# The last chunk of two streamed tensors (H's sixteenth, G's eleventh) starts 64 bytes further on

## The chip, the cores and the metric

The kernel runs on one core of a Trainium2 chip. The metric is the device time of one execution in microseconds (us); less is better. Engines are TensorE (PE in the profile, its weight loads PEld), VectorE (DVE), ScalarE (ACT), GpSimd (POOL) and SyncE (SP), which issues the weight transfers.

## The reference

A sequence of 256 tokens of width 2048 goes through two blocks of two layers each, in float32. What matters here is that nearly all of the arithmetic is products of the 2048-wide activations with large weight matrices:

```python
def first_block(x, p, positions, ...):
    for i in range(DEPTH):
        h = rmsnorm(x, g_mix[i])
        z = h @ w_in[i]
        ...
        y = jnp.concatenate([y_a, y_b, y_c, y_d], axis=-1) @ w_o[i]
        x = x + y
        uf = causal_dwconv(rmsnorm(x, g_ffn[i]) @ w_up[i], w_ffn_conv[i])
        gate, up = jnp.split(uf, 2, axis=-1)
        x = x + (jax.nn.silu(gate) * up) @ w_down[i]
        pe_gate = jax.nn.sigmoid(rmsnorm(x, g_pe[i]) @ w_pg[i])
        x = x + (p[i] @ w_pe[i]) * pe_gate
    return x
```

Between `w_in` and `w_o` stand an attention, a gated convolution, a longer convolution and a retention; their 512-wide outputs are joined. The second block (`hybrid_layer`) has the same frame: a norm, one projection `w_in`, four mixers (three kinds of attention and a gated linear attention) and `w_out`. It ends with a norm of x.

## The kernel before

Activations lie with channels on the 128 partitions: a tensor of 2048 channels is 16 chunks (`DC`) of 128 channels by T = 256 tokens. To get float32 precision, each operand is split in two parts in the type float32r, a high part and the remainder. `H` holds the operand of the current product, 16 chunks of 512 columns: columns 0 to 255 of a chunk are its high part (written by ScalarE, L1226, L1236, L1338, L1356 or L1502) and columns 256 to 511 the low part (written by VectorE, L1686 or L1697). `G` holds the same for the gated FFN activation, two buffers of 11 chunks (`GC`); its parts are written by ScalarE (L1564) and GpSimd (L514).

Weights come in slabs, one slab for each 128 output channels: 16 blocks (11 for `down`) of 128 x 128. SyncE loads a slab into `raw`, a ring of 4; ScalarE copies it to `whi` (L1164); VectorE writes the remainder to `wlo` (L1630), which takes the place of `raw`. TensorE goes through the slabs one after another. `run` is the loop over the slabs of one product. For each slab of the kind `streams_both` it does two passes over the chunks into one PSUM bank: in the first, block k of `whi` is the loaded weight and all 512 columns of chunk k are streamed (L642); in the second, block k of `wlo` is loaded and the 256 high columns are streamed (L653). Each matmul has its own weight load. Then VectorE adds the bank's halves and takes the result out, while TensorE is at the next slab. The first two slabs behind a norm are done in another order by `high_first` (L585, L587: whi and wlo blocks in turn on the high part; L596: whi on the low part, 32 in a row). `value_slab` (L676 to L678) loads pieces of `H` as weights and streams `whi` and `wlo`. `both_units` (L703 to L707) streams `pT_hl` in halves of 256 columns, with whi, whi and wlo in turn, right ahead of the product `pg`. Small matmuls of the attentions are put between the slabs of `zq` to `rg` and `gla` to `gates`, and ahead of the last quarter of their first pass.

The product `wout` takes its chunks in the order `Y_ORDER[1]` (0 to 9, 12 to 15, 10, 11), that is how they come ready; the parameter `order` of `run` hands it over (L631, L649).

SBUF is laid out in the order of the allocations. Three unused tensors stand between them and shift what follows: `ahead_of_raw` (320 bytes a partition), `ahead_of_whi` (192 bytes) and `ahead_of_z` (416 bytes). A chunk of H or G is 2048 bytes, a weight block 512 bytes. In the built program the start addresses in a partition are H 32896, raw and wlo 65984, whi 98944, pT_hl 149312, G and z 179840, cq 212608. By "line parity" the change means whether such an address divided by 64 is even or odd.

Of the kernel before, what the change touches and what calls it, by code (L numbers as in the profile page):

```python
# [27 lines left out]
P = 128  # L28
T = 256
# [226 lines left out]
def _build(nc, d, out, ctx):  # L256
    def sb(name, shape, dt=F32):
        return ctx.enter_context(nc.sbuf_tensor(name, shape, dt))
# [3 lines left out]
    H = sb("H", [P, DC, 2 * T], F32R)  # L262
    sb("ahead_of_raw", [P, 80])
# [48 lines left out]
    G = ctx.enter_context(nc.sbuf_tensor("G", [P, 2, GC, 2 * T], F32R))  # L312
    ctx.enter_context(nc.sbuf_tensor("rest_of_y", [P, 48 * T - 2 * GC * 2 * T], F32))
# [148 lines left out]
    def _(pool):  # L462
# [36 lines left out]
        def activations(l, g):  # L499
# [4 lines left out]
            for i, j in groups(pool, r, 2):  # L504
# [8 lines left out]
                gg = G[:, g % 2, bass.ds(pair, 1), :].rearrange("p a t -> p (a t)")  # L513
# [49 lines left out]
    def _(pe):  # L563
# [6 lines left out]
        def high_first(key, h_base, order, middle):  # L570
# [4 lines left out]
            for u in range(2):  # L575
# [5 lines left out]
                for k in chunks:  # L581
# [3 lines left out]
                    pe.matmul(b[:, 0:T], whi[:, n % RAW, w], r.src[:, k, 0:T], start=k == chunks[0], stop=False,  # L585
                              skip_group_check=True)
                    pe.matmul(b[:, 0:T], wlo[:, n % RAW, w], r.src[:, k, 0:T], start=False, stop=k == chunks[-1],  # L587
                              skip_group_check=True)
            middle()
            for u in range(2):  # L590
                n = r.first + u
                b = bank_of(r, n)
                for k in chunks:
                    if u == 0:
                        pe.wait_ge(S("h_ready"), h_base + rank[k] + 1)
                    last = pe.matmul(b[:, T:2 * T], whi[:, n % RAW, k * r.m:(k + 1) * r.m], r.src[:, k, T:2 * T],  # L596
# [3 lines left out]
        def run(key, operand=None, beside=None, base=None, free=None, order=None, high=None, middle=None):  # L600
# [5 lines left out]
            for i, j in groups(pe, r, 0):  # L606
# [21 lines left out]
                for first in range(0, r.kt, step):  # L628
                    chunks = range(first, min(first + step, r.kt))
                    for at in chunks:  # L630
                        k = at if order is None else order[at]  # L631
# [9 lines left out]
                        if both:  # L641
                            pe.matmul(b[0:r.m, :], whi[:, n % RAW, w], r.src[:, k, :], start=at == 0, stop=False)  # L642
                        else:
                            pe.matmul(b[0:r.m, 0:T], whi[:, n % RAW, w], r.src[:, k, 0:T], start=at == 0, stop=False)
                            pe.matmul(b[0:r.m, 0:T], whi[:, n % RAW, w], r.src[:, k, T:2 * T], start=False, stop=False)
                    if both and not opening and first == 0:
                        pe.wait_ge(S("lo_ready"), n + 4 * i + 1)
                    for at in chunks:
                        k = at if order is None else order[at]  # L649
# [3 lines left out]
                        last = pe.matmul(b[0:r.m, 0:T], wlo[:, n % RAW, w], r.src[:, k, 0:T], start=False,  # L653
# [8 lines left out]
        def value_slab(r, g):  # L662
# [5 lines left out]
            for kk in range(4):  # L668
# [4 lines left out]
                for t in range(2):  # L673
                    b = bank_of(r, n0 + t)
                    high, low = (r.src[:, k, o + t * P:o + (t + 1) * P] for o in (0, T))
# [13 lines left out]
        def both_units(l):  # L689

            r = by["pe", l]
            for u in range(2):
                n = r.first + u
                pe.wait_ge(S("lo_ready"), n + 1)
                for p in range(4):
# [3 lines left out]
                    for o in range(2):  # L699
                        dst = b[:, o * T:(o + 1) * T]  # L700
                        for k in range(2):
                            w = slice(8 * P * k + P * (2 * p + o), 8 * P * k + P * (2 * p + o + 1))
                            pe.matmul(dst, whi[:, n % RAW, w], r.src[:, k, 0:T], start=k == 0, stop=False,  # L703
# [1579 lines left out]
```

## Time and profile before

| | us |
|---|---|
| median of 3 runs | 3352.53 (3350.43 to 3353.65) |
| profiled execution | 3352.41 |
| its span in the trace | 3350.2 |
| PE busy in the span | 3327.6 (99%) |
| DVE busy | 2617.8 (78%) |
| ACT busy | 1531.6 (46%) |
| POOL busy | 864.2 (26%) |

The profile page gives busy times, shares in 40 equal slices, the waits, and the costliest groups of instructions by line of the kernel. Matmuls overlap one another: each takes longer from its start to its end than the next one's start lags behind its own. So a group's mean says little of the pace; the timeline does. It merges instructions of the same kind into one row with the start of the first, the time from there to the end of the last, and their count. A window that is cut short shows the first few of a longer row.

### The profile page before, as it was taken

Reading aid. Unit: us, or ns where it says so; the run is one execution under the profiler, and the core shown is the slowest. Engines: PE = TensorE matmul, PEld = TensorE weight load, DVE = VectorE, ACT = ScalarE, POOL = GpSimd, SP = SyncE. Lnnn points to the kernel's source line nnn. Section 1 sums busy time; section 2 is a strip of 40 time slices with the busy share of each in tenths; the row PEclk is TensorE's granted clock in tenths of the full one; section 3 lists DMA queues with packets and bytes.
Section 4 is the critical chain, followed back from the end, with each engine's and each line's share of the span. In section 5 each row is a group of like instructions: output and inputs, shape, how many; then the busy total and the mean of one; then the engine's idle time right before and its main releaser. Section 6 shows DMA issues by size and latency. Waiting matters only on the chain. (4 is left out here: it accounts for less than half of the span.)

```text
span 3350.2 us, 53769 instructions
## 1 busy us (share of the span) xinstructions
PE 3327.6 (99%) x20366; PEld 2929.1 (87%) x20366; DVE 2617.8 (78%) x3394; ACT 1531.6 (46%) x1642; POOL 864.2 (26%) x633
## 2 busy tenths in 40 slices
PE   9999999999999999999999999999999999999998
PEld 8989888888888989888888888888888888888897
DVE  8897788787786888887887787867867866678865
ACT  5644444343433556544443434335444444445443
POOL 0422432121122423414332121214432004150004
PEclk9999999999999999999999999999999999999999
DMA  6445555555555554455555555555544455544454
GB/s 241 148 163 176 189 188 189 178 202 177 206 174 189 203 182 165 151 176 187 190 188 178 198 180 199 180 190 200 193 164 153 167 173 189 180 164 151 167 185 151
DMA packets 90647, 605.21 MB, mean 181 GB/s; under 512 B 10192, under 2 KB 10352, under 8 KB 29296
## 3 DMA queue, kind: packets, MB, share of 16 engines
q1 hardware_dynamic: 89424, 599.83, 52.0%
q10 hardware_dynamic: 1056, 3.11, 0.2%
q8 instruction: 110, 1.80, 0.2%
q14 instruction: 57, 0.47, 0.0%
HBM read 600.80 MB, written 2.10 MB: 180 GB/s over the span
## 5 line engine op out<-in xcount | busy, mean ns | idle before, releaser
L642 PE MATMUL bank<-H,whi 128*128 128x512 f32 x6496 | 1574.3, 393 | 1.5 <-DVE z L1661 1.5
L1164 ACT ACTIVATE whi<-raw 128x2048 fp32r<-128x2048 f32 (+2 forms) x609 | 1093.6, 1796 | 1044.6 <-DMA raw<-in_slabs_down 259.8
L1630 DVE TENSOR_TENSOR wlo<-raw,whi 128x2048 fp32r<-128x2048 f32 (+2 forms) x609 | 1328.4, 2181 | 243.2 <-ACT whi L1164 233.1
L642 PEld LDWEIGHTS bank<-H,whi 128*128 128x128 f32 x6496 | 1188.7, 188 | 238.6 <-issue 5.9
L653 PEld LDWEIGHTS bank<-H,wlo 128*128 128x128 f32 x6624 | 849.1, 188 | 34.3
L653 PE MATMUL bank<-H,wlo 128*128 128x256 f32 x6624 | 871.1, 281 | 0.0
L511 POOL TENSOR_TENSOR sqtmp<-tmp 128x256 f32<-128x256 f32 x88 | 218.9, 2488 | 867.8 <-DVE tmp L2211 867.8
L642 PE MATMUL bank<-G,whi 128*128 128x512 f32 x1408 | 343.0, 391 | 0.0
L642 PEld LDWEIGHTS bank<-G,whi 128*128 128x128 f32 x1408 | 255.4, 188 | 48.0
L1564 ACT ACTIVATE G<-sqtmp 128x256 f32 (+1 forms) x88 | 36.8, 418 | 404.0 <-POOL sqtmp L511 404.0
L489 POOL TENSOR_TENSOR sqacc<-sqacc,sqtmp 128x256 f32<-128x256 f32 x119 | 199.4, 1676 | 9.4
L1651 DVE TENSOR_REDUCE tmp<-bank 128x256 f32<-128x512 f32 x216 | 149.0, 690 | 65.9 <-PE bank L653 65.4
L484 POOL TENSOR_TENSOR sqtmp<-x 128x256 f32<-128x256 f32 x119 | 133.7, 1123 | 238.5 <-DVE x L1705 182.5
L653 PEld LDWEIGHTS bank<-G,wlo 128*128 128x128 f32 x1408 | 184.3, 189 | 9.8
L529 POOL TENSOR_TENSOR z<-z,y 128x255 f32<-128x255 f32 (+14 forms) x120 | 121.1, 1009 | 269.9 <-ACT y L1381 254.2
L1704 DVE TENSOR_TENSOR x<-x,bank 128x256 f32 (+1 forms) x192 | 80.7, 420 | 138.8 <-PE bank L653 138.7
L653 PE MATMUL bank<-G,wlo 128*128 128x256 f32 x1408 | 186.8, 281 | 0.0
L1651 DVE TENSOR_REDUCE z<-bank 128x256 f32<-128x512 f32 x132 | 91.0, 690 | 103.1 <-PE bank L653 102.0
L484 POOL TENSOR_TENSOR sqacc<-x 128x256 f32<-128x256 f32 x8 | 16.3, 2031 | 589.0 <-DVE x L1705 547.1
L676 PE MATMUL bank<-whi,H 128*128 128x512 f32 x320 | 129.9, 406 | 0.0
L678 PE MATMUL bank<-whi,H 128*128 128x512 f32 x320 | 126.1, 394 | 0.0
L677 PE MATMUL bank<-wlo,H 128*128 128x512 f32 x320 | 126.0, 394 | 0.0
(390 smaller groups left out, 2881.4 us busy)
## 6 DMA issues: line engine op xcount, KB each, us to landing
raw<-in_slabs_up SPq DMA_DIRECT2D x176, 1024.0 KB, 4.8
raw<-in_slabs_down SPq DMA_DIRECT2D x128, 704.0 KB, 4.0
raw<-in_slabs_wo SPq DMA_DIRECT2D x32, 1024.0 KB, 4.8
raw<-in_slabs_pg SPq DMA_DIRECT2D x32, 1024.0 KB, 4.9
raw<-in_slabs_gates SPq DMA_DIRECT2D x32, 1024.0 KB, 4.9
raw<-in_slabs_wout SPq DMA_DIRECT2D x32, 1024.0 KB, 4.8
raw<-in_slabs_sc SPq DMA_DIRECT2D x24, 1024.0 KB, 4.8
raw<-in_slabs_fox SPq DMA_DIRECT2D x24, 1024.0 KB, 4.9
```

The source lines that it names most:

```text
L484: pool.tensor_tensor((sqtmp if c else sqacc)[:], x[:, c, :], x[:, c, :], ALU.mult).then_inc(S("pool_sq"), 1)
L489: ins = pool.tensor_tensor(sqacc[:], sqacc[:], sqtmp[:], ALU.add)
L511: pool.tensor_tensor(act_f[:], tmp[:, 3, :], tmp[:, 2, :], ALU.mult).then_inc(S("act_f32"), 1)
L529: pool.tensor_tensor(o[:, s:T], o[:, s:T], product[:, done["tap"] % TAP_RING, s:T], ALU.add).then_inc(S("cf_pool"), 1)
L642: pe.matmul(b[0:r.m, :], whi[:, n % RAW, w], r.src[:, k, :], start=at == 0, stop=False)
L653: last = pe.matmul(b[0:r.m, 0:T], wlo[:, n % RAW, w], r.src[:, k, 0:T], start=False, stop=at == r.kt - 1)
L676: pe.matmul(b[:], high, whi[:, n % RAW, w], start=k == 0, stop=False)
L677: pe.matmul(b[:], high, wlo[:, n % RAW, w], start=False, stop=False)
L678: last = pe.matmul(b[:], low, whi[:, n % RAW, w], start=False, stop=k == DC - 1)
L1164: act.activation(whi[:, n % RAW, 0:w], raw[:, n % RAW, 0:w], ACT.Copy).then_inc(S("hi_ready"), 1)
L1630: dve.tensor_tensor(wlo[:, n % RAW, 0:w], raw[:, n % RAW, 0:w], whi[:, n % RAW, 0:w].bitcast(F32), ALU.subtract).then_inc(S("lo_ready"), 1)
L1651: return dve.tensor_reduce(dst, b[0:m, :].rearrange("p (h t) -> p t h", h=2), AX, ALU.add)
```

## The change

H and G lose their last chunk, which becomes a tensor of its own behind 64 unused bytes (16 float32). The pad behind H shrinks by the same 64 bytes, so raw, wlo, whi and all that follows stay where they were; the 64 bytes behind G come out of the unused rest of that area. H's chunk 15 starts at byte 63680 instead of 63616, and G's chunk 10 at 220864 and 222912. G's second buffer of ten chunks starts at 200320 instead of 202368. H becomes a list of chunks, and `r.src[:, k, ...]` is written `r.src[k][:, ...]` in all its uses; `g_chunk` picks a chunk of G. The slabs of `wo` and `wout` behind the first two no longer follow `order`, but go through the chunks from 0 to 15; for `wo` this is the same. The count of instructions, their sizes and their waits stay.

```diff
--- before.py
+++ after.py
@@ -259,8 +259,11 @@
 
 
     x = sb("x", [P, DC, T])
-    H = sb("H", [P, DC, 2 * T], F32R)
-    sb("ahead_of_raw", [P, 80])
+    H_most = sb("H", [P, DC - 1, 2 * T], F32R)
+    sb("ahead_of_H_last", [P, 16])
+    H_last = sb("H_last", [P, 2 * T], F32R)
+    H = [H_most[:, c, :] for c in range(DC - 1)] + [H_last[:]]
+    sb("ahead_of_raw", [P, 64])
     area_raw = nc.sbuf_tensor("raw", [P, RAW, 2048], F32)
     raw = area_raw.__enter__()
     area_raw.__exit__(None, None, None)
@@ -309,8 +312,16 @@
     cq = area_cq.__enter__()
     area_cq.__exit__(None, None, None)
     area.__exit__(None, None, None)
-    G = ctx.enter_context(nc.sbuf_tensor("G", [P, 2, GC, 2 * T], F32R))
-    ctx.enter_context(nc.sbuf_tensor("rest_of_y", [P, 48 * T - 2 * GC * 2 * T], F32))
+    G = sb("G", [P, 2, GC - 1, 2 * T], F32R)
+    sb("ahead_of_G_last", [P, 16])
+    G_last = sb("G_last", [P, 2, 2 * T], F32R)
+    sb("rest_of_y", [P, 48 * T - 2 * GC * 2 * T - 16])
+
+    def g_chunk(g, pair):
+
+        if isinstance(pair, int):
+            return G_last[:, g % 2, :] if pair == GC - 1 else G[:, g % 2, pair, :]
+        return G[:, g % 2, bass.ds(pair, 1), :].rearrange("p a t -> p (a t)")
 
     bank = [ctx.enter_context(nc.psum_tensor(f"bank{b}", [P, 512], F32)) for b in range(4)]
     pS = ctx.enter_context(nc.psum_tensor("pS", [P, 512], F32))
@@ -339,13 +350,14 @@
 
     HANDED = ("wo", "pg", "wout", "rg", "gates")
     runs, by, h_free = [], {}, {}
-    sources = {"qn": cq, "qr": cq, "kv": cq[:, 4:6, :]}
+    latent = [cq[:, c, :] for c in range(6)]
+    sources = {"qn": latent[0:4], "qr": latent[0:4], "kv": latent[4:6]}
     for key, _, _, kt, m, count, _, _ in slab_table():
         src = sources.get(key[0], H)
         if key[0] == "down":
-            src = G[:, key[2] % 2]
+            src = [g_chunk(key[2], c) for c in range(GC)]
         elif key[0] == "pe":
-            src = pT_hl[:, key[1]]
+            src = [pT_hl[:, key[1], c, :] for c in range(2)]
         loop = key[0] in ("wo", "up", "down", "pg", "wout")
         by[key] = Run(d[slab_name(key)], kt, m, count, src, loop, sum(r.count for r in runs))
         if key[0] in ("pg", "wo", "wout") or key[0] == "up" and key[2] == 0:
@@ -510,7 +522,7 @@
                 pool.wait_ge(S("g_ready"), 1 + base + pair)
                 pool.tensor_tensor(act_f[:], tmp[:, 3, :], tmp[:, 2, :], ALU.mult).then_inc(S("act_f32"), 1)
                 pool.wait_ge(S("g_hi"), base + pair + 1)
-                gg = G[:, g % 2, bass.ds(pair, 1), :].rearrange("p a t -> p (a t)")
+                gg = g_chunk(g, pair)
                 pool.tensor_tensor(gg[:, T:2 * T], act_f[:], gg[:, 0:T].bitcast(F32),
                                    ALU.subtract).then_inc(S("g_ready"), 1)
 
...
@@ -628,7 +640,7 @@
                 for first in range(0, r.kt, step):
                     chunks = range(first, min(first + step, r.kt))
                     for at in chunks:
-                        k = at if order is None else order[at]
+                        k = at
                         if opening and at == 0:
                             pe.wait_ge(S("h_ready"), 8)
                         if opening and at % 4 == 0:
...
@@ -639,18 +651,18 @@
                             operand(k)
                         w = slice(k * r.m, (k + 1) * r.m)
                         if both:
-                            pe.matmul(b[0:r.m, :], whi[:, n % RAW, w], r.src[:, k, :], start=at == 0, stop=False)
+                            pe.matmul(b[0:r.m, :], whi[:, n % RAW, w], r.src[k], start=at == 0, stop=False)
                         else:
-                            pe.matmul(b[0:r.m, 0:T], whi[:, n % RAW, w], r.src[:, k, 0:T], start=at == 0, stop=False)
-                            pe.matmul(b[0:r.m, 0:T], whi[:, n % RAW, w], r.src[:, k, T:2 * T], start=False, stop=False)
+                            pe.matmul(b[0:r.m, 0:T], whi[:, n % RAW, w], r.src[k][:, 0:T], start=at == 0, stop=False)
+                            pe.matmul(b[0:r.m, 0:T], whi[:, n % RAW, w], r.src[k][:, T:2 * T], start=False, stop=False)
                     if both and not opening and first == 0:
                         pe.wait_ge(S("lo_ready"), n + 4 * i + 1)
                     for at in chunks:
-                        k = at if order is None else order[at]
+                        k = at
                         w = slice(k * r.m, (k + 1) * r.m)
                         if at == (r.kt // 4 if step == r.kt else r.kt * 6 // 8):
                             advance(beside, 1)
-                        last = pe.matmul(b[0:r.m, 0:T], wlo[:, n % RAW, w], r.src[:, k, 0:T], start=False,
+                        last = pe.matmul(b[0:r.m, 0:T], wlo[:, n % RAW, w], r.src[k][:, 0:T], start=False,
                                          stop=at == r.kt - 1)
                         if handed and at in (3, 7, 11):
                             last.then_inc(S("h_free"), 1)
...
@@ -1683,7 +1695,7 @@
             h0 = DC * ((cnt["h"] if lo else nth("h")) - 1)
             for c in range(lo, hi):
                 dve.wait_ge(S("h_hi"), h0 + c + 1)
-                dve.scalar_tensor_tensor(H[:, c, T:2 * T], x[:, c, :], col(g, l, c), H[:, c, 0:T].bitcast(F32),
+                dve.scalar_tensor_tensor(H[c][:, T:2 * T], x[:, c, :], col(g, l, c), H[c][:, 0:T].bitcast(F32),
                                          ALU.mult, ALU.subtract).then_inc(S("h_ready"), 1)
 
         def scaled(dst, b, m=P):
```

The other hunks put `r.src[k][:, ...]` for `r.src[:, k, ...]`, `H[c][:, ...]` for `H[:, c, ...]` and `g_chunk(...)` for an indexed G in the same way.

## Rows read from the trace of the kernel before

**Rows 1.** The page's head, busy shares, and granted clock in 40 slices.
```profile
span 3350.2 us, 53769 instructions
PE 3327.6 (99%) x20366; PEld 2929.1 (87%) x20366; DVE 2617.8 (78%) x3394; ACT 1531.6 (46%) x1642; POOL 864.2 (26%) x633
...
PEclk9999999999999999999999999999999999999999
```

**Rows 2.** Waits of PE, the longest: total us, times, longest us.
```profile
PE pX L1085 <- ACT whi L1520: 5.0, 1, 5.0
```

**Rows 3.** The page's groups of L642 and L653: count, busy us, mean ns.
```profile
L642 PE MATMUL bank<-H,whi 128*128 128x512 f32 x6496 | 1574.3, 393 | 1.5 <-DVE z L1661 1.5
...
L653 PE MATMUL bank<-H,wlo 128*128 128x256 f32 x6624 | 871.1, 281 | 0.0
...
L642 PE MATMUL bank<-G,whi 128*128 128x512 f32 x1408 | 343.0, 391 | 0.0
```

**Rows 4.** Timeline of PE, one slab on H: start us, length us, line, count.
```profile
1803.26 3.82 PE L642 MATMUL bank<-H,whi 128*128 128x512 f32 x16
1806.91 2.05 PE L653 MATMUL bank<-H,wlo 128*128 128x256 f32 x16
1808.80 2.68 PE L642 MATMUL bank<-G,whi 128*128 128x512 f32 x11
```

**Rows 5.** Timelines of PE and PEld in windows that cut this first pass short.
```profile
1803.26 1.55 PE L642 MATMUL bank<-H,whi 128*128 128x512 f32 x6
...
1803.26 2.23 PE L642 MATMUL bank<-H,whi 128*128 128x512 f32 x9
...
1803.14 1.00 PEld L642 LDWEIGHTS bank<-H,whi 128*128 128x128 f32 x5
```

**Rows 6.** Timeline of PE behind high_first: L596 and the slab after it.
```profile
291.90 4.00 PE L596 MATMUL bank<-H,whi 128*128 128x256 f32 x32
295.74 3.82 PE L642 MATMUL bank<-H,whi 128*128 128x512 f32 x16
299.39 0.28 PE L653 MATMUL bank<-H,wlo 128*128 128x256 f32 x1
```

**Rows 7.** Timeline of PE behind both_units, in three windows; the last is layer 1.
```profile
1116.92 0.28 PE L707 MATMUL pX<-pT_hl,wlo 128*128 128x256 f32 x1
1117.04 3.79 PE L642 MATMUL bank<-H,whi 128*128 128x512 f32 x16
1120.66 2.05 PE L653 MATMUL bank<-H,wlo 128*128 128x256 f32 x16
...
1117.04 2.20 PE L642 MATMUL bank<-H,whi 128*128 128x512 f32 x9
...
2307.97 3.79 PE L642 MATMUL bank<-H,whi 128*128 128x512 f32 x16
```

**Rows 8.** Timeline of the other engines at 1803 and at 1117.
```profile
1802.99 1.36 ACT L1164 ACTIVATE whi<-raw 128x1408 fp32r<-128x1408 f32 x1
...
1803.46 0.69 DVE L1651 TENSOR_REDUCE tmp<-bank 128x256 f32<-128x512 f32 x1 [1.43 <-PE bank L653]
...
1116.51 1.92 ACT L1164 ACTIVATE whi<-raw 128x2048 fp32r<-128x2048 f32 x1
...
1117.48 0.68 DVE L2219 COPY z<-bank 128x512 f32<-128x512 f32 x1
```

**Rows 9.** Busy us of each engine in 300 us of up and down.
```profile
1700.00:2000.00 300.00, 300.00 (x1736) 265.02 (x1735) 242.50 (x307) 118.69 (x103) 72.27 (x44) 1.00 0.54 187
```

**Rows 10.** Timeline of PE, a second pass behind a first pass cut by attention matmuls.
```profile
206.15 1.18 PE L642 MATMUL bank<-H,whi 128*128 128x512 f32 x4
207.17 1.99 PE L653 MATMUL bank<-H,wlo 128*128 128x256 f32 x16
```

**Rows 11.** Timeline of PE behind a value slab.
```profile
185.19 3.79 PE L642 MATMUL bank<-H,whi 128*128 128x512 f32 x16
188.82 2.05 PE L653 MATMUL bank<-H,wlo 128*128 128x256 f32 x16
```

More of the change, by code:

```diff
@@ L584, in high_first @@
                     w = slice(k * r.m, (k + 1) * r.m)
-                    pe.matmul(b[:, 0:T], whi[:, n % RAW, w], r.src[:, k, 0:T], start=k == chunks[0], stop=False,
+                    pe.matmul(b[:, 0:T], whi[:, n % RAW, w], r.src[k][:, 0:T], start=k == chunks[0], stop=False,
                               skip_group_check=True)
-                    pe.matmul(b[:, 0:T], wlo[:, n % RAW, w], r.src[:, k, 0:T], start=False, stop=k == chunks[-1],
+                    pe.matmul(b[:, 0:T], wlo[:, n % RAW, w], r.src[k][:, 0:T], start=False, stop=k == chunks[-1],
                               skip_group_check=True)
@@ L595, in high_first @@
                         pe.wait_ge(S("h_ready"), h_base + rank[k] + 1)
-                    last = pe.matmul(b[:, T:2 * T], whi[:, n % RAW, k * r.m:(k + 1) * r.m], r.src[:, k, T:2 * T],
+                    last = pe.matmul(b[:, T:2 * T], whi[:, n % RAW, k * r.m:(k + 1) * r.m], r.src[k][:, T:2 * T],
                                      start=k == chunks[0], stop=k == chunks[-1], skip_group_check=True)
@@ L674, in value_slab @@
                     b = bank_of(r, n0 + t)
-                    high, low = (r.src[:, k, o + t * P:o + (t + 1) * P] for o in (0, T))
+                    high, low = (r.src[k][:, o + t * P:o + (t + 1) * P] for o in (0, T))
                     pe.matmul(b[:], high, whi[:, n % RAW, w], start=k == 0, stop=False)
@@ L702, in both_units @@
                             w = slice(8 * P * k + P * (2 * p + o), 8 * P * k + P * (2 * p + o + 1))
[L703 removed]
+                            pe.matmul(dst, whi[:, n % RAW, w], r.src[k][:, 0:T], start=k == 0, stop=False,
                                       skip_group_check=True)
[L705 removed]
+                            pe.matmul(dst, whi[:, n % RAW, w], r.src[k][:, T:2 * T], start=False, stop=False,
                                       skip_group_check=True)
[L707 removed]
+                            last = pe.matmul(dst, wlo[:, n % RAW, w], r.src[k][:, 0:T], start=False, stop=k == 1,
                                              skip_group_check=True)
@@ L744, in pair_unit @@
                         w = slice(r.m * k + P * (2 * p + o), r.m * k + P * (2 * p + o + 1))
-                        pe.matmul(dst, whi[:, n % RAW, w], r.src[:, k, 0:T], start=k == 0, stop=False,
+                        pe.matmul(dst, whi[:, n % RAW, w], r.src[k][:, 0:T], start=k == 0, stop=False,
                                   skip_group_check=True)
-                        pe.matmul(dst, whi[:, n % RAW, w], r.src[:, k, T:2 * T], start=False, stop=False,
+                        pe.matmul(dst, whi[:, n % RAW, w], r.src[k][:, T:2 * T], start=False, stop=False,
                                   skip_group_check=True)
-                        last = pe.matmul(dst, wlo[:, n % RAW, w], r.src[:, k, 0:T], start=False, stop=k == r.kt - 1,
+                        last = pe.matmul(dst, wlo[:, n % RAW, w], r.src[k][:, 0:T], start=False, stop=k == r.kt - 1,
                                          skip_group_check=True)
```

16 lines of the change are left out of this document (7 added, 9 removed).

## The prediction, made before the kernel after was run

> **What bounds the kernel now.** I read the page's busy shares first, then the waits of TensorE, then its costliest groups, then its timeline in narrow windows, then the timeline of all engines. The shares say TensorE: 3327.6 of 3350.2 us busy, the next engine at 78%, the granted clock in the top tenth in every slice (so 2.4 GHz but for the first and last microseconds) [rows 1]. Its longest wait on anybody is 5.0 us, once [rows 2]. So only what one matmul costs in the stream of matmuls can move the time. The groups name the stream: per slab 16 matmuls of 512 columns with weights from whi (I call it the high pass) and 16 of 256 columns with weights from wlo (the low pass), 11 and 11 where G is streamed; 6496/16 = 406 such slabs on H and 1408/11 = 128 on G, 534 in all [rows 3]. The means in these rows (393, 281 ns) overlap one another; what counts is start to start, which the timeline gives.
>
> **One slab, start to start.** A high pass on H starts at 1803.26 and its low pass at 1806.91: 3.65 us for 16. The low pass ends at the next start, 1808.80: 1.89 us for 16, 118 ns each [rows 4]. The high pass isn't even. Its first six span 1.55 us; a row ends 0.39 us after its last start (the row that ends with the pass: 3.82 us long, next start after 3.65, and a mean of 0.39 in the groups), so five steps take 1.16 us, 232 ns each. The other eleven take 3.65 - 1.16 = 2.49 us, 226.4 ns each [rows 3 to 5]. So every high pass pays about 5 x (232 - 226.5) = 0.027 us at its start. That is 0.03 us that steady streaming doesn't need.
>
> **What the change touches.** It adds no instruction, no wait and no transfer. In the built program of before H starts at byte 32896, wlo at 65984, whi at 98944, pT_hl at 149312, G at 179840, cq at 212608; divided by 64 these are even, odd, even, odd, even, even, and chunks (2048 or 1024 bytes) and weight blocks (512 bytes) keep their tensor's parity. The change makes H's chunk 15 and G's chunk 10 odd; everything else stays where it was or keeps its parity. The weight load of matmul k+1 starts with the stream of matmul k: the first whi load of the pass at 1803.26 starts at 1803.14, one low step ahead of it [rows 5]. So each stream runs beside a load, and a pair can have the same parity or different ones:
> - high pass, chunks 0 to 14: H even, whi even: same. Low pass, chunks 0 to 14: H even, wlo odd: different. Unchanged.
> - last of the high pass, beside the first wlo load: different before, same after.
> - last of the low pass, beside the next slab's first whi load: same before, different after.
> - chunk 14 beside the load for chunk 15: unchanged, the weights don't move.
>
> So the change makes each pass keep its own relation up to its last matmul. The order argument that it drops in wout's later slabs also makes the last chunk there 15 instead of 11, so those slabs take part too; their waits are unchanged, cost 0.
>
> **Does the parity matter?** The trace has two passages that are near to the changed one.
> - 32 matmuls of 256 columns on H with whi weights (same parity, L596) take 295.74 - 291.90 = 3.84 us, 120.0 ns each; the low pass with wlo weights takes 118 [rows 4, 6]. So a same-parity pair costs about 2 ns more at this width. Behind them the high pass again takes 3.65 us (295.74 to 299.39): slow start.
> - Behind the pT_hl unit the last 256-column stream is odd beside an even whi load, which is exactly the pair that the change makes. There the high pass takes 1120.66 - 1117.04 = 3.62 us, and its first nine span 2.20 us where the ordinary one's span 2.23 [rows 5, 7]. The slow start is gone; the second pT_hl unit, in the other layer, shows the same. Both stretches have the same neighbours: VectorE reads the bank just finished and ScalarE writes whi at 1803 and at 1117 alike [rows 8]. So the slow start isn't their doing, and goes with what streamed last.
>
> Sum. High pass: 3.65 - 3.62 = 0.03 us by the rows; 0.027 by the steps above. Last low matmul: 120 to 118, 0.002. Last high matmul turns from different to same: bound by the same 2 ns as a loss, 0.001 taken. So 0.027 to 0.03, taken 0.028 us for each high pass that follows directly on a low pass ending in the moved chunk. Counting these through the timeline of the span gives 319 behind H and 126 behind G, 445 of 534; the others have attention matmuls ahead of them, or are cut in fours, and keep what they have. 445 x 0.028 = 12.5 us. Cover: none is needed, TensorE is the bound; VectorE is busy 242.5 us of 300 in an up/down stretch [rows 9], so 0.4% less TensorE time doesn't make it late. The profiled run took 3352.41 us around a span of 3350.2, and the median of before is 3352.53, 0.12 more. 3352.4 - 12.5 = **3340 us**.
>
> **The unobserved side.** No passage of before has a 512-column stream in a same-parity pair directly ahead of a low pass. What this does to the low pass has to be bounded from both sides, and the low pass is sensitive: behind a high pass of four that is itself still in its slow start, 16 low matmuls span 1.99 us instead of 2.05 [rows 4, 10], (1.99 - 0.28)/15 = 114.0 ns each instead of 118.0. So there are at least two steady paces, and which one is caught hangs on how the pass is entered. Upper bound: the pace of L596, 120, or a slow start like the high pass's. I take zero, because the low pass starts at 118 now after a high pass that is steady when it ends, and a last high matmul that stays steady resembles that most.
>
> **A rule against.** By the rows, 256-column steps of 120 and 118 ns differ only in which weights are loaded beside them. The Trainium skill (TensorE: Matmul & The Clock Gate, "Part 2: What happens when you issue a matmul") says that the engine reads the stream and the weights through two independent ports, and that loading the next weights takes nothing from the running matmul; by that rule alone the change is worth 0 and the sum 3352.4. It is rival 1, and the 2 ns and the 0.03 us speak against it as far as two passages can.
>
> **Rivals.**
> 1. No effect, or trading one slow start for another (20%): the slow start is a property of entering 512 columns from 256, and the pT_hl unit escapes it since it mixes weights and halves. For it: all 445 passes are entered in that one way, and the pT_hl unit is met only twice. Against: the high pass behind a value slab, entered from a same-parity 512-column stream, takes 188.82 - 185.19 = 3.63 us [rows 11], and the one behind L596, all one kind of weights, still has the slow start, so the last stream does matter. Time: 3352, or 3347 to 3357 with small changes.
> 2. The low pass gets worse (slower, 22%): the last high stream now shares its parity with the first wlo load, and the low pass goes at L596's pace. Price: 2 ns x 16 x about 396 + 2 ns x 11 x 128 = 15.5 us; or a slow start of 0.028 us x 524 = 14.7 us. With the gain kept: 3352.4 - 12.5 + 15 = 3355. With the gain missing: 3367. It decides from 12.5/524 = 24 ns per slab, 1.5 ns per low matmul, on. I give 6% to the two cancelling (within 0.2%), 16% to slower by over 0.2%.
> 3. The low pass falls into the pace of 114 (9%): 4 ns x 16 x 396 + 4 ns x 11 x 128 = 31 us beyond the gain: 3309; half of the slabs, 3325.
> 4. The sum itself, 3334 to 3345: 49%.
>
> **How the numbers follow.** Likeliest 3340. What can be told from no change here is about 0.2%, 6.7 us: faster below 3345.7, slower above 3359.1. Faster: 49 + 9 + 1 of rival 1 = 59%. Slower: 16 + 2 of rival 1 = 18%. Same: the rest, 23%. The range runs from 3324, which takes in half of rival 3, to 3360, which takes in rival 1 and the cancelling part of rival 2; the rest of rival 3 and of rival 2 stay out, some 19%. The likeliest case alone is 3334 to 3345.
>
> **What the profile after would show.** Right: ordinary high passes of 3.62 us instead of 3.65, their first nine spanning 2.20; the low pass still 1.88 to 1.89 us; the group rows of L642 with the same counts; the saving spread over all stretches by their number of slabs and largest in up and down. Rival 1: 3.65 stays. Rival 2: low passes at 1.91 to 1.92 or an uneven start in them. Rival 3: low passes at 1.82. What would make me wrong: the parity isn't what the chip sees (another address bit), or the odd chunk behind an even one (or the even one behind an odd one) costs something of its own, twice per pass, in which case steps 14 to 15 and 15 to 0 are long; 6 ns each would take back the whole gain.

## The result, and the profile after

The kernel after takes 3358.78 us (median of 21 runs, 3356.62 to 3363.3) against 3352.09 for the kernel before, run beside it. The ratio is 1.0021, 95% interval 1.0014 to 1.0027: slower by 0.2%, where I forecast 0.4% faster. The profiled execution took 3358.79 us around a span of 3356.6, 6.4 us more than the span of before.

Part of the scatter from execution to execution is TensorE's granted clock. Beside the f runs below, before took 3350.1 us (median of 10) at a mean clock of 0.999 and 3352.3 (median of 17) at 0.998. In its profiled execution the clock was 0.66 from 116 to 121 us, so it stood at 1.2 GHz in part of that window, and the matmuls there took 5.97 us where they took 4.41 in after. After has two such places, at 144 to 149 and at 1328 to 1333 us, also 0.66.

TensorE is still the bound, and nothing new waits. The head of the page, busy shares and granted clock:

```profile
span 3356.6 us, 53769 instructions
PE 3335.2 (99%) x20366; PEld 2927.2 (87%) x20366; DVE 2616.7 (78%) x3394; ACT 1531.5 (46%) x1642; POOL 866.2 (26%) x633
...
PEclk9999999999999999999999999999999999999999
```

The longest waits of PE (total us, times, longest us):

```profile
PE pX L1097 <- ACT whi L1532: 5.1, 1, 5.1
PE pX L944 <- POOL w L561: 3.1, 6, 0.8
```

Counts, slices of the clock and the longest wait are those of [rows 1] and [rows 2], within 0.1 us; lines from 640 on have moved by 12, so L654 and L665 are the high and the low pass. The loss is in the steps. The timeline of PE, one ordinary slab on H and one on G (start us, length us, line, count); the moved chunk now has a row of its own:

```profile
1801.74 3.61 PE L654 MATMUL bank<-H,whi 128*128 128x512 f32 x15
1805.18 0.39 PE L654 MATMUL bank<-H_last,whi 128*128 128x512 f32 x1
1805.41 1.93 PE L665 MATMUL bank<-H,wlo 128*128 128x256 f32 x15
1807.18 0.28 PE L665 MATMUL bank<-H_last,wlo 128*128 128x256 f32 x1
1807.30 3.61 PE L654 MATMUL bank<-H,whi 128*128 128x512 f32 x15
...
1812.86 2.47 PE L654 MATMUL bank<-G,whi 128*128 128x512 f32 x10
1815.17 0.39 PE L654 MATMUL bank<-G_last,whi 128*128 128x512 f32 x1
1815.40 1.34 PE L665 MATMUL bank<-G,wlo 128*128 128x256 f32 x10
1816.58 0.28 PE L665 MATMUL bank<-G_last,wlo 128*128 128x256 f32 x1
1816.69 2.45 PE L654 MATMUL bank<-G,whi 128*128 128x512 f32 x10
```

On H the high pass takes 1805.41 - 1801.74 = 3.67 us where [rows 4] has 3.65, and the slab 1807.30 - 1801.74 = 5.56 where [rows 4] has 5.54. Windows that cut the pass short show where:

```profile
1801.74 1.55 PE L654 MATMUL bank<-H,whi 128*128 128x512 f32 x6
...
1801.74 2.25 PE L654 MATMUL bank<-H,whi 128*128 128x512 f32 x9
```

Six span 1.55 us as in [rows 5], but nine span 2.25 instead of 2.23: the slow start is not gone, it lasts longer. Start to start, the median over the 291 ordinary high passes on H, worked out from the whole timeline of each kernel, in ns:

```
before  233 236 228 232 231 227 227 227 227 227 227 227 ... 227 226
after   232 233 236 224 231 236 228 233 231 227 227 227 ... 227 232
```

The sequence 231, 236, 228, 232 or 233, 231, 227 is the same in both; only the first step differs from it in before. After enters it four steps earlier, which costs 16 ns a pass, and its last step takes 232 ns instead of 226. The low pass is 2 ns shorter. So a slab of H takes 20 ns more. On G the last high step costs 6 ns more too, but the last low step takes 113 ns instead of 118, and the slow start is unchanged: 3.813 us a slab in both.

One more loss lies where attention matmuls cut the high pass and its last four matmuls run in the slow start. The low pass behind them, timeline of PE of after:

```profile
206.91 1.93 PE L665 MATMUL bank<-H,wlo 128*128 128x256 f32 x15
208.68 0.28 PE L665 MATMUL bank<-H_last,wlo 128*128 128x256 f32 x1
```

(1.93 - 0.28)/14 = 118 ns a step, where [rows 10] had 114. There are 36 such passes; 34 had the pace of 114 in before and 10 have it in after, so 24 lost it, at 0.05 us each 1.2 us. Moving the last high stream of H is enough for that: in e5 below, where nothing else moves, 10 of the 36 have it too, and in e1, where only the last low stream moves, 34.

The estimate by units is 319 x 0.020 = 6.4 us on H, 0 on G and 1.2 in the cut passes, 7.6; the span grew by 6.4. Step by step over the whole span, matmul for matmul, the difference divides so: H's other passes +5.8 us, G's +0.1, the cut low passes +1.2, the places with a lower clock +1.5 (two instead of one), 42 steps of over 0.4 us -0.8, and all other matmuls -1.5; 6.3 in sum.

### The profile page after: what moved, and what is told of

Same layout as the page of the kernel before. It is cut to its first block and busy times, and to the rows that moved or that the text cites. A ratio compares the mean times of both kernels' runs of the same rounds, so it can differ in the third digit from the quotient of the medians.

```text
span 3356.6 us, 53769 instructions
## 1 busy us (share of the span) xinstructions
PE 3335.2 (99%) x20366; PEld 2927.2 (87%) x20366; DVE 2616.7 (78%) x3394; ACT 1531.5 (46%) x1642; POOL 866.2 (26%) x633
## 5 line engine op out<-in xcount | busy, mean ns | idle before, releaser
L654 PE MATMUL bank<-H,whi 128*128 128x512 f32 (+1 forms) x6090 | 1486.8, 394 | 1.2 <-ACT whi L1176 0.4
L654 PEld LDWEIGHTS bank<-H,whi 128*128 128x128 f32 (+1 forms) x6090 | 1110.4, 188 | 228.6 <-issue 3.9
L665 PEld LDWEIGHTS bank<-H,wlo 128*128 128x128 f32 (+1 forms) x6210 | 801.7, 189 | 36.6
L665 PE MATMUL bank<-H,wlo 128*128 128x256 f32 (+1 forms) x6210 | 822.3, 281 | 0.0
L654 PE MATMUL bank<-G,whi 128*128 128x512 f32 x1280 | 314.2, 391 | 0.0
L654 PEld LDWEIGHTS bank<-G,whi 128*128 128x128 f32 x1280 | 230.8, 188 | 43.1
L665 PEld LDWEIGHTS bank<-G,wlo 128*128 128x128 f32 x1280 | 169.0, 189 | 10.5
L665 PE MATMUL bank<-G,wlo 128*128 128x256 f32 x1280 | 171.4, 281 | 0.0
L654 PE MATMUL bank<-H_last,whi 128*128 128x512 f32 (+1 forms) x406 | 159.5, 393 | 0.0
L688 PE MATMUL bank<-whi,H 128*128 128x512 f32 x300 | 122.0, 407 | 0.0
L690 PE MATMUL bank<-whi,H 128*128 128x512 f32 x300 | 118.2, 394 | 0.0
```

Source lines behind the costliest of these rows:

```text
L654: pe.matmul(b[0:r.m, :], whi[:, n % RAW, w], r.src[k], start=at == 0, stop=False)
L665: last = pe.matmul(b[0:r.m, 0:T], wlo[:, n % RAW, w], r.src[k][:, 0:T], start=False, stop=at == r.kt - 1)
L688: pe.matmul(b[:], high, whi[:, n % RAW, w], start=k == 0, stop=False)
L690: last = pe.matmul(b[:], low, whi[:, n % RAW, w], start=False, stop=k == DC - 1)
```

## The experiments

In the e runs and in g2 the layout stays that of before, but for e4, e5 and e8, and a single stream of each pass (in e3 every stream of the low pass) is started at another address by taking it some columns later or earlier in the tensor. These kernels (not e4 and e8) compute with shifted data. The time of a step doesn't show that: the last high step takes 232 ns in e5 as in after, and 237 in e2 as in f3, where the data are the right ones. The f runs and g1 are after with other shifts. `flat` is H, or G's buffer, as one row of columns; 16 columns are 64 bytes.

### Each moved place alone: e1 and e2

```diff
 e1: low pass
-last = pe.matmul(..., r.src[:, k, 0:T], ...)
+last = pe.matmul(..., flat[:, 512 * k + s:512 * k + s + T], ...)   # s = 16 if at == r.kt - 1 else 0
 e2: high pass
-pe.matmul(..., r.src[:, k, :], ...)
+pe.matmul(..., flat[:, 512 * k + s:512 * k + s + 512], ...)        # s = -16 if at == r.kt - 1 else 0
```

> The layout of before; only the last matmul of each low pass (chunk 15 of H, chunk 10 of G, 256 columns) streams from 64 bytes further on, so that its start is odd; the data streamed there are shifted by 16 columns. Theory A (the two moved streams act each by itself, and the odd last low stream is what enters H's high pass earlier in its slow start): ordinary H high passes take 3.67 us instead of 3.65, their last step stays at 226 ns, G's last low step falls to 113 ns; 319 x 0.016 us = +5 us on H, 128 x 0.005 = 0.6 us less on G, together 3356 to 3357. Rival B (the longer slow start comes from the last high stream, through the phase that the low pass inherits): high passes stay at 3.65 us and the time at 3352 or 0.6 us less. The theory of the prediction (the odd last low stream removes the slow start): high passes of 3.62 us, 3340.

Measured: 3354.14 us, ratio 1.0009 (1.0000 to 1.0019). The odd last low stream alone gives H a slab of 5.540 us, the same as before, though by other steps: the last low step takes 122 ns instead of 120 and the next high pass starts 230, 224, 231, 236, 228. On G it enters the slow start where after has it on H (232, 233, 236, 224, ...), 3.833 us a slab. So theory A had the mechanism on the wrong tensor. Rival B's forecast holds for the length of H's high pass (3.652 us), but not for its steps and not on G. The prediction's own theory falls: no ordinary high pass lost its slow start. The 2.4 us that e1 takes more than before (3351.71, run beside it) are G's: 126 x 0.020 = 2.5.

> The layout of before; only the last matmul of each high pass (512 columns) streams from 64 bytes further back, so that its start is odd; the data streamed there are shifted by 16 columns. Theory A: its step takes 232 ns instead of 226, nothing else moves: 534 x 0.0056 = +3.0 us, 3355. Rival B: the step of 232 and, behind the low pass, a high pass that starts earlier in its slow start, 3.67 us before its last step: 3.0 + 4.5 = 7.5 us, 3360, so that this one place explains the whole loss.

Measured: 3355.60 us, ratio 1.0012 (1.0002 to 1.0021). The last high step takes 237 ns, not 232, and behind the low pass the next high pass starts with 231 instead of 233 on H. Neither expectation fits: 64 bytes back isn't 64 bytes on. H's slab takes 5.547 us.

### Steady parity: e3 and e4

```diff
 e3: low pass, every chunk
+last = pe.matmul(..., flat[:, 512 * k + 16:512 * k + 16 + T], ...)
 e4: layout
+sb("ahead_of_H", [P, 16])
 H = sb("H", [P, DC, 2 * T], F32R)
-sb("ahead_of_raw", [P, 80])
+sb("ahead_of_raw", [P, 64])
```

> The layout of before; every matmul of each low pass streams from 64 bytes further on (data shifted by 16 columns), so that all its starts are odd like the wlo blocks loaded beside them. If same parity costs 2 ns at this width in itself (the reading of L596): low steps of 120 ns, 7904 x 2.3 ns = +18 us, 3370. If the L596 pace came from something else (whi blocks, the low half streamed): low steps stay at 117.5 and the time within 3350 to 3357. If what cleared the slow start behind pT_hl was a run of odd streams and not one: high passes of 3.62 us here, 12 us less than either.

Measured: 3365.64 us, ratio 1.0047 (1.0030 to 1.0063). The timeline of PE in e3:

```profile
1804.42 3.82 PE L647 MATMUL bank<-H,whi 128*128 128x512 f32 x16
1808.08 2.07 PE L658 MATMUL bank<-H,wlo 128*128 128x256 f32 x16
1809.99 3.37 PE L647 MATMUL bank<-H,whi 128*128 128x512 f32 x14
```

The low pass takes 1.91 us instead of 1.89; from its seventh step on each takes 120 ns. The reading of L596 holds, somewhat less than priced because the first six steps are uneven (116 to 121). The high pass takes 3.66: a run of odd streams doesn't clear the slow start either.

> H as a whole is moved on by 64 bytes, G, raw, wlo and whi stay where they are; nothing is left out. High passes on H then pair odd streams with even whi loads, low passes odd streams with odd wlo loads. If the parity of stream and load sets the pace: high steps of 224 ns instead of 226.7 (the pace of a last step, 225.8, or less) and low steps of 120 instead of 117.5, in sum 406 x 16 x (2.3 - 0.9 to 2.7) ns: between 3350 and 3361, with G's passes as before. If only changes of parity between one stream and the next matter: H's passes keep 226.7 and 117.5 with the slow start unchanged, 3352 within 2 us.

Measured: 3366.40 us, ratio 1.0044 (1.0027 to 1.0061). Low steps on H take 120 ns. High steps go 226, 229, 232 in turn, 229 on average against 226.7, with no slow start at all, 3.660 us a pass. At 256 columns the four pairs are now complete. Stream even beside load even (L596) takes 120 ns and odd beside odd (the low passes of e3 and e4) 120 too; even beside odd (low pass of before) takes 117.5 and odd beside even (e4's L597, which is L596 of before) 118. So there the pair decides, and not the address of the stream alone. For steady high passes only two pairs were run, both with whi even: the same-parity pair of before is better by 2.3 ns. The layout of before has the better one of both widths. That the high step would get shorter was wrong. The 225.8 ns of a last high step isn't the pace of such pairs, it is a single step out of step.

### Does parity decide? e5, e6, e7

```diff
 e5: H with 16 spare columns, ahead_of_raw 16 shorter; high pass on H only
+pe.matmul(..., H_flat[:, 512 * k + s:512 * k + s + 512], ...)      # s = 16 if at == r.kt - 1 else 0
 e6, e7: as e1 with s = 32 (128 bytes) and s = 8 (32 bytes)
```

> The layout of before; only on H, the last matmul of each high pass streams from 64 bytes further on, as after does (in e2 it was 64 bytes back, and its step took 237 ns where after's takes 232). Data shifted by 16 columns. If the two moves act each by itself: the last high step takes 232 ns, +2.3 us over 406 slabs, the next high pass starts as before (233, 236, 228, 232, 231 ns), and e5 and e1 add up to after: 3354.5. If they act through the phase that the low pass hands on: the last low step or the first high steps change too, by some 2 to 16 ns per slab, up or down, and the sum of e1 and e5 isn't after. If 64 back and 64 on are the same to the chip (parity alone decides), the last step takes 237 ns again.

Measured: 3353.02 us, ratio 1.0003 (0.9994 to 1.0013). The last high step takes 232 ns as in after, the low pass is 4 ns shorter, and the next high pass starts with 231 instead of 233. H's slab: 5.540 us, as before. So on H neither move alone costs a slab anything, and both together cost 20 ns. The last low step and the next high pass change here although their own addresses don't: something is handed on from step to step.

> As e1_low_last with 128 bytes instead of 64, so that the last low stream starts even again (data shifted by 32 columns). If line parity is what the chip sees: steps and high passes of before (last low step 120 ns on H, 118 on G; high passes start 233, 236 on H and 231, 236 on G). If the length of the jump or a higher address bit matters: other values.

Measured in one run: 3351.88 us. The start is even again, and yet H's high pass enters its slow start late (232, 232, 231, 227) and takes 3.641 us, and G's enters it early and takes 2.539. The timeline of PE in e6:

```profile
1803.28 3.80 PE L647 MATMUL bank<-H,whi 128*128 128x512 f32 x16
1806.92 2.05 PE L658 MATMUL bank<-H,wlo 128*128 128x256 f32 x16
1808.81 2.67 PE L647 MATMUL bank<-G,whi 128*128 128x512 f32 x11
```

Line parity alone isn't what decides at the last step of a pass.

> As e1_low_last with 32 bytes: the start lies in the middle of a line, and 17 lines are touched. If only the parity of the line of the first byte matters: the steps of before. If the place in the line matters: last low step between 118 and 124 ns and the next high pass entered at another point of its slow start, -5 to +18 ns per slab.

Measured in one run: 3354.99 us. H's last low step takes 125 ns and the high pass starts 224, 231, 236; the slab again takes 5.540 us. The place in the line matters for single steps; over the slab it comes out even. (The 3354.99 is no sign of more: the mean clock of this execution was 0.997, and that of before took 3355.5 us at 0.997, median of three beside it.)

### The passage that the prediction rested on: e8

```diff
+sb("ahead_of_pT", [P, 16])
 pT_hl = sb("pT_hl", [P, L, 2, 2 * T], F32R)
+sb("behind_pT", [P, 48])
...
-sb("ahead_of_z", [P, 104])
+sb("ahead_of_z", [P, 40])
```

> Only pT_hl moves on by 64 bytes (tensors between it and z by 256, z and all else stay); nothing is left out. It tests the step of the prediction on which the gain stood. If the odd last stream behind both_units was what spared the next high pass its slow start, that pass now takes 3.65 us like the others. If it was something else in that passage (streams of whi, whi and wlo in turn), it still takes 3.62 us. The time is that of before in both cases, since there are only two such passes.

Measured in one run: 3351.28 us. The timeline of PE in e8, then the same place in after, where pT_hl is odd as it was before:

```profile
1115.31 0.28 PE L709 MATMUL pX<-pT_hl,wlo 128*128 128x256 f32 x1
1115.43 3.81 PE L644 MATMUL bank<-H,whi 128*128 128x512 f32 x16
1119.08 1.10 PE L655 MATMUL bank<-H,wlo 128*128 128x256 f32 x8
```

and in after:

```profile
1118.65 0.28 PE L719 MATMUL pX<-pT_hl,wlo 128*128 128x256 f32 x1
1118.77 3.60 PE L654 MATMUL bank<-H,whi 128*128 128x512 f32 x15
1122.21 0.39 PE L654 MATMUL bank<-H_last,whi 128*128 128x512 f32 x1
1122.44 0.75 PE L665 MATMUL bank<-H,wlo 128*128 128x256 f32 x5
```

With pT_hl even the pass has its slow start, 3.65 us: the line did matter there. But in after, with pT_hl odd as in [rows 7], the pass also has a slow start and takes 3.67. So an odd last stream clears it in one course of steps and not in another. What sets the course lies further back. In f1 below, which differs from after only in G's last chunk, the slow start is absent again, in both layers; the timeline of PE in f1:

```profile
1118.53 0.28 PE L718 MATMUL pX<-pT_hl,wlo 128*128 128x256 f32 x1
1118.65 3.56 PE L653 MATMUL bank<-H,whi 128*128 128x512 f32 x15
1122.05 0.39 PE L653 MATMUL bank<-H_last,whi 128*128 128x512 f32 x1
1122.28 0.99 PE L664 MATMUL bank<-H,wlo 128*128 128x256 f32 x7
```

The high pass takes 1122.28 - 1118.65 = 3.63 us, 6 ns of it the longer last step. Between G's last low stream and this pass lie the 96 matmuls of both_units, some 11 us, with the same addresses in both kernels. Their steps run through one repeating series from 114 to 124 ns, and the pass meets it at another point: the last steps ahead of it are 118, 117, 121, 116 in f1 and 117, 116, 119, 114 in after. The other runs agree: the pass is free of the slow start in before, e5, f1, f4 and g3, where G's last low stream is unmoved or 256 on, and has it in e1, e3, e7, f2, f3, g1 and g2, where it is moved. Only e6 doesn't fit this, where it is moved by 128 and the pass stays free. (Counted by the first of the two such passes in e1 and g1, whose second starts with a longer step; e2, e4 and e8 are left out.)

### After with other shifts: f1 to f4, g1

```diff
 f1: H 64 bytes, G 0      f2: both 128      f3: both 192      f4: both 256      g1: H 128, G 192
-sb("ahead_of_H_last", [P, 16])
+sb("ahead_of_H_last", [P, h])
-sb("ahead_of_raw", [P, 64])
+sb("ahead_of_raw", [P, 80 - h])
-sb("ahead_of_G_last", [P, 16])
+sb("ahead_of_G_last", [P, g])
```

> After with G's last chunk put back to an even line (its two last chunks stay a tensor of their own behind the others). H's chunk 15 stays 64 bytes on. If H alone brings the loss: slabs of H as in after (high pass 3.675 us, low pass 1.885), slabs of G as in before (2.518 and 1.296), and the time is after's, 3358 to 3360, since G's slabs took 3.81 us in both. If the jump to the chunk matters rather than its line (G's buffer 0 now jumps over buffer 1), G's last steps change by some ns although every start is even.

Measured: 3359.76 us, ratio 1.0021 (1.0012 to 1.0030), the whole loss. H's slabs are those of after, G's those of before, although G's first buffer now jumps over its second to reach its last chunk. H alone makes the loss, and the jump's length doesn't show in the ordinary slabs.

> After with both last chunks 128 bytes on instead of 64: all starts are even again. If line parity is what the chip sees, all steps are those of before and the time is 3352. If the bytes count beyond parity, as e6 showed for the low pass alone (H's high pass 3.641 us instead of 3.653, G's 2.539 instead of 2.518), other values: with the low pass's effect alone, H gains 0.013 us x 319 and G loses 0.021 us x 126, 3351; the last high step, not measured at 128, moves by 0 to 6 ns, 0 to +3 us, and shifts where the low pass's pattern ends, 5540 ns a slab plus or minus 20: 3345 to 3360.

Measured: 3346.64 us, ratio 0.9980 (0.9971 to 0.9989): faster than before. The timeline of PE in f2, whole and in a window that cuts the pass short:

```profile
1798.42 3.56 PE L654 MATMUL bank<-H,whi 128*128 128x512 f32 x15
1801.82 0.40 PE L654 MATMUL bank<-H_last,whi 128*128 128x512 f32 x1
1802.05 1.93 PE L665 MATMUL bank<-H,wlo 128*128 128x256 f32 x15
1803.82 0.28 PE L665 MATMUL bank<-H_last,wlo 128*128 128x256 f32 x1
1803.94 2.43 PE L654 MATMUL bank<-G,whi 128*128 128x512 f32 x10
...
1798.42 1.52 PE L654 MATMUL bank<-H,whi 128*128 128x512 f32 x6
```

Six span 1.52 us where [rows 5] has 1.55: here H's slow start is gone (226 or 227 ns from the first step on). It gives 28 ns a pass; the last high step, 234 ns, takes back 8. The slab takes 5.520 us.

> After with both last chunks 192 bytes on: all parities are those of after. If line parity decides, every step and the time are after's: last high step 232 ns, H's high pass 3.675 us, 3358.8. If not, a slab of H takes something else than 5.560 us (5.520 to 5.570 by what the other shifts gave) and the time lies between 3344 and 3362.

Measured: 3356.04 us, ratio 1.0015 (1.0006 to 1.0024). H's slab takes 5.560 us as in after, with a last high step of 237, the same as in e2, and -64 and 192 differ by 256. G's slow start is gone instead of H's: 3.800 us a slab.

> After with both last chunks 256 bytes on: all parities are those of before. If 256 bytes are a period of what the chip sees, or parity alone counts, every step is that of before (high pass 233, 236, 228, 232, 231 ns first, last step 226, low pass ending in 120), 3352. If the jump itself costs, whatever its length, the last step of the high pass is longer than 226 ns and the time above 3353.

Measured: 3352.18 us, ratio 1.0000 (0.9991 to 1.0009), with every step of the ordinary slabs within 1 ns of before (233, 236, 228, 233, 231 first, 226 last). For this stream 256 bytes on are as good as none, and splitting the tensors costs nothing.

> After with H's last chunk 128 bytes on and G's 192, each the best shift that the runs so far show for its tensor. If a slab's time depends only on its own tensor's shift: H as in f2 (5.520 us a slab), G as in f3 (2.506 + 1.294 = 3.800 us against 3.813 in f2), so 128 x 0.013 = 1.7 us less than f2, 3345. If passes of H and G disturb one another where they meet, G's gain is missing or H's smaller: 3347 to 3352.

Measured: 3345.36 us, ratio 0.9980 (0.9971 to 0.9989), the fastest kernel here; its profiled span is 3341.3 against 3343.5 in f2. The timeline of PE in g1:

```profile
1796.87 3.56 PE L654 MATMUL bank<-H,whi 128*128 128x512 f32 x15
1800.26 0.40 PE L654 MATMUL bank<-H_last,whi 128*128 128x512 f32 x1
1800.50 1.93 PE L665 MATMUL bank<-H,wlo 128*128 128x256 f32 x15
...
1802.38 2.43 PE L654 MATMUL bank<-G,whi 128*128 128x512 f32 x10
1804.65 0.40 PE L654 MATMUL bank<-G_last,whi 128*128 128x512 f32 x1
1804.89 1.34 PE L665 MATMUL bank<-G,wlo 128*128 128x256 f32 x10
1806.07 0.28 PE L665 MATMUL bank<-G_last,wlo 128*128 128x256 f32 x1
1806.18 2.43 PE L654 MATMUL bank<-G,whi 128*128 128x512 f32 x10
```

A slab of G takes 1806.18 - 1802.38 = 3.80 us, and H keeps its 5.520: the ordinary slabs of the two tensors don't disturb one another. The timed difference to f2, 1.3 us, is within the scatter of both; at a mean clock of 0.999 the medians of three executions each are 3343.5 and 3345.1, 1.6 apart where 1.7 was expected.

### What was left: g2 and g3

```diff
 g2: as e1 with s = 48 (192 bytes)
 g3: before, in run, both passes
-k = at if order is None else order[at]
+k = at
```

> The layout of before; only the last stream of each low pass starts 192 bytes further on (data shifted by 48 columns). It separates the two places for the shift that takes G's slow start away in f3. If the last low stream does it alone: G's high pass 2.50 us here too, H's 3.67 or so as in f3. If it takes both places together, through the pattern of the low pass: G's and H's high passes are other than in f3, as e6 (G 2.539, H 3.641) differs from f2 (2.515, 3.633).

Measured in one run: 3346.05 us. With the last low stream alone at 192, it is H whose slow start goes (one step of 233, then 227), 5.520 us, and G has an early entry, 3.827. In f3, with both places at 192, it was the other way round. It takes both places together.

> Before with only the order of wout's later slabs dropped, the one part of the change that no other run has alone: the last chunk there is 15 instead of 11, both even, and chunks 10 and 11 are no longer behind 15. If it costs nothing, as the prediction had it: 3352 and wout's high passes at 3.653 us. If the jump back and forth or the last chunk's place matters: wout's 28 slabs change by up to 20 ns each, 0.6 us, still within what can't be told from no change.

Measured: 3351.80 us, ratio 1.0002 (0.9993 to 1.0012); the ordinary high passes take 3.653 us. The dropped order has no part in the loss.

### The shifts in one table

Medians over the ordinary passes and slabs, in ns, worked out from the timelines; "last" is the last step. The slab is taken from start to start of two high passes. f1 is after on H and before on G, g1 is f2 on H and f3 on G.

| run | moved, bytes | H high (last) | H low (last) | H slab | G slab |
|---|---|---|---|---|---|
| before, f4 | 0, both 256 | 3653 (226) | 1887 (120) | 5540 | 3813 |
| e5 | H high 64 | 3657 (232) | 1883 (118) | 5540 | 3813 |
| e1 | low 64 | 3652 (226) | 1888 (122) | 5540 | 3833 |
| after | both 64 | 3675 (232) | 1885 (120) | 5560 | 3813 |
| e7 | low 32 | 3648 (226) | 1892 (125) | 5540 | 3813 |
| e6 | low 128 | 3641 (226) | 1886 (119) | 5527 | 3833 |
| f2 | both 128 | 3633 (234) | 1887 (119) | 5520 | 3813 |
| g2 | low 192 | 3632 (226) | 1888 (121) | 5520 | 3827 |
| e2 | high -64 | 3662 (237) | 1884 (118) | 5547 | 3827 |
| f3 | both 192 | 3676 (237) | 1884 (118) | 5560 | 3800 |

## Why the prediction was wrong

- **TensorE is the bound, and only steps can move the time:** right. No count changed, and the two longest waits of PE stayed at 5.0 to 5.1 and 3.1 to 3.4 us. (A misreading without weight: the clock was below 2.4 GHz near 118 us too, which 40 slices are too coarse to show.)
- **A same-parity pair costs 2 ns in the low pass:** right for a whole pass (e3 and e4, 120 against 117.5 ns). For the single last step it failed: with an odd last stream H's took 120 (after) or 122 (e1), G's 113 or 120. A single step isn't priced by the pace of a steady pass. Nor is every steady pass: twice in e3 an odd low pass beside odd loads goes at 113.3 ns.
- **The last high step, 0.001 us:** wrong in size. It rose by 6 ns, 534 x 0.006 = 3 us. It was bounded by a pace, too. The prediction named steps that are 6 ns longer at the moved chunk as a sign of being wrong; one of the four steps that it named, the one from the high pass's chunk 15 to the low pass's chunk 0, is that much longer.
- **The slow start goes when the last low stream is odd beside an even load:** this is the step that failed, and 12 of the 12.5 us stood on it. It rested on one passage, pT_hl, met twice. That passage is real, and its parity does matter (e8), but the same pair in another course of steps has the slow start (after, behind pT_hl; e1 and e3, everywhere), and f1 shows that what decides there was streamed 96 matmuls earlier. What counts is at which point of its sequence the high pass is entered. That hangs on the last high stream, on the course of the low pass behind it, and on the last low stream together (e1 and e5 against after; g2 against f3). The two stretches had the same pair; I took them to be in the same state.
- **What comes next:** I had rivals in which the slow start stays, or the low pass gets one, but none in which the high pass enters its own earlier. That is what H does in after: 16 ns a pass lost, where 27 were to be gained. G shows that it needn't: there after gave back exactly what it took.
- **The low pass keeps 118:** right for ordinary passes (1.885 us). For the cut passes it failed: 24 of 36 lost the pace of 114, 1.2 us. I had read that pace as something to be gained and didn't ask whether it could be lost.
- **No cost of other parts** (order, split tensors, G's buffers): right (g3, f4, f1).
- **The rule against:** the Trainium skill (TensorE: Matmul & The Clock Gate, "Part 2: What happens when you issue a matmul") says that stream and weights are read through two independent ports and that loading takes nothing from the running matmul; by that alone nothing should have changed. Here it doesn't hold to the last percent: the 256-column step takes 120 or 118 ns by the pair of stream and load (e3, e4), and between layouts with the same instructions a slab took from 5.520 to 5.573 us (f2 and e4), 1%.

The measured 3358.8 lies within the range, near its upper end, 0.3 us below the time from which I called it slower (18%). That the range holds it is luck: its upper end was there for rival 1 and for a slower low pass cancelling the gain, and the mechanism measured is neither.

What stays open is why a shift acts as it does. The runs show sequences and their entry points, not what is being waited for inside a step. Nor do they show why the state outlasts 96 matmuls behind pT_hl. The loads' addresses were never moved, whole passes only by 64 bytes, and the period of 256 rests on f4 and on the last high step of e2 and f3.

## What to carry to other kernels

In this kernel, where TensorE streams without a gap, a change of address was worth tenths of a percent either way, and its sign couldn't be had from a similar passage elsewhere: steps follow one another in a sequence with a memory, so the same pair of addresses costs differently in another course. Read start to start, not mean durations, over a whole repeating unit, and price the unit, since a gain in one step often comes back in the next (5.540 us a slab of H came out of four different courses: before, e5, e1, e7). Such offsets are cheaper to scan than to argue: here 0, 64, 128 and 192 bytes cover the period of 256, and H and G could be chosen apart.

## What the runs showed of the hardware

- With the same instructions, weights and clock, the step from one 512-column matmul to the next is 224 to 238 ns, and the 256-column step 113 to 125, by start addresses and by what streamed before (medians of the ordinary passes of all runs).
- A high pass has one sequence at its start, ... 233 236 224 231 236 228 232 231 227 227 ..., entered at different points; the first one or two steps can differ from it (e6: 232 233 231 227). 288 of 291 ordinary high passes on H in before follow it within 2 ns, whatever VectorE and ScalarE do beside them. With all of H 64 bytes on (e4) it is gone, and 226 229 232 repeats.
- The last high step rises with the shift of its stream: 226, 232, 234 and 237 ns at 0, 64, 128 and 192 bytes, and 226 again at 256 (before, after, f2, f3, f4).
- What an earlier address sets up can last: with another last chunk of G (f1 against after) the high pass 96 matmuls later takes 3.63 us instead of 3.67, in both layers.
- At 256 columns a steady step takes 120 ns where stream and load have the same line parity and 117.5 to 118 where they don't, in all four pairs (L596 and low pass of before, low pass and L597 of e4).
- Slab times come in steps: 5520, 5527, 5540, 5547, 5560 on H and 3800, 3813, 3827, 3833 on G are all within 1 ns of multiples of 6.67 ns, 16 periods of a 2.4 GHz clock.
- There is a faster steady pace of the low pass, 113.3 ns. It was seen behind high passes that hadn't settled at 227 ns when they ended: behind 34 cut ones in before, behind none of the ordinary ones, and behind two in e3, although the parities of stream and load are the same there.
